# Summing the modulation's partitions with ones as the weights, and the products moved to the front of the mixers' stage

## The reference, cut to what matters

```python
for l in range(DEPTH):                                   # DEPTH = 2
    mod = cond @ ada_w[l] + ada_b[l]                     # 1024 -> 6 * 1024
    sh1, sc1, g1, sh2, sc2, g2 = jnp.split(mod, 6, axis=-1)
    h = rms_norm(x, norm1_g[l]) * (1.0 + sc1) + sh1
    pa, pb, pc, pd = split(h @ w_in[l], GROUP_COLS)
    y = concatenate([rwkv7(pa), diff_attention(pb), spatial_gating(pc), forgetting_attention(pd)])
    x = x + g1 * (y @ w_out[l])
    h = rms_norm(x, norm2_g[l]) * (1.0 + sc2) + sh2
    x = x + g2 * conv_glu_ffn(h)
...
mod = silu(c) @ w_mod + b_mod                            # second block: the same for a GLA mixer
x = x + g1 * gla(h, h_ctx)
x = x + g2 * moe(modulate(rmsnorm(x), sh2, sc2))
```

## Time and profile before

| | |
|---|---|
| Median of 3 runs | 2577.76 us (2577.53 to 2583.84) |
| Profiled execution, its own time | 2571.56 us |
| Its span in the trace | 2569.8 us |
| PE busy | 2306.9 us (90%) |
| PE weight loads busy | 1853.0 us (72%) |
| DVE busy | 1598.1 us (62%) |
| ACT busy | 1067.6 us (42%) |
| POOL busy | 177.1 us (7%) |

### The profile page before, as it was taken

One profiled execution on the slowest core, in us unless ns is written; L12 is line 12 of the kernel. 1 busy time (PEld: TensorE's weight loads), 2 busy tenths in 40 slices (PEclk: granted clock), 3 DMA queues, 4 the chain that ended last, 5 costly groups with the idle time before them and its releaser, 6 DMA issues. The chain is left out here.

```text
span 2569.8 us, 32135 instructions
## 1 busy us (share of the span) xinstructions
PE 2306.9 (90%) x11490; PEld 1853.0 (72%) x11490; DVE 1598.1 (62%) x2270; ACT 1067.6 (42%) x1616; POOL 177.1 (7%) x201
## 2 busy tenths in 40 slices
PE   4998689799999999877989999999998888799995
PEld 3777566578888777756657888788877776677774
DVE  6654656555567565565655555774643655699996
ACT  3443244333342234242343333423333434577774
POOL 0001100000000000111000000000000101123232
PEclk8998899999999999799989999998999999899997
DMA  7640000222225355100012223445624001799995
GB/s 295 219 164 5 1 34 1 78 79 97 90 100 188 112 196 190 44 1 1 34 42 75 97 90 101 153 150 182 210 92 164 1 1 43 291 397 397 396 397 213
DMA packets 95240, 348.22 MB, mean 136 GB/s; under 512 B 12288, under 2 KB 14352, under 8 KB 94864
## 3 DMA queue, kind: packets, MB, share of 16 engines
q1 hardware_dynamic: 88496, 323.57, 35.4%
q0 software_dynamic: 3888, 14.16, 1.4%
q10 hardware_dynamic: 2736, 8.92, 0.9%
HBM read 333.50 MB, written 21.50 MB: 138 GB/s over the span
## 5 line engine op out<-in xcount | busy, mean ns | idle before, releaser
L498 PE MATMUL ps<-a_hi,w_hi 128*128 128x512 f32 x1408 | 572.8, 407 | 41.6 <-DVE y_lo L1775 18.4
L500 PE MATMUL ps<-a_hi,w_lo 128*128 128x512 f32 x1408 | 564.6, 401 | 0.0
L499 PE MATMUL ps<-h_lo,w_hi 128*128 128x512 f32 x1280 | 508.2, 397 | 0.0
L462 DVE TENSOR_TENSOR w_lo<-ring,w_hi 128x1024 fp32r<-128x1024 f32 x178 | 218.1, 1226 | 384.3 <-ACT w_hi L457 383.9
L457 ACT ACTIVATE w_hi<-ring 128x1024 fp32r<-128x1024 f32 x178 | 188.3, 1058 | 532.8 <-PE ps L500 520.1
L498 PEld LDWEIGHTS ps<-a_hi,w_hi 128*128 128x128 f32 x1408 | 268.9, 191 | 115.7 <-DVE w_lo L462 28.4
L500 PEld LDWEIGHTS ps<-a_hi,w_lo 128*128 128x128 f32 x1408 | 268.5, 191 | 66.6
L499 PEld LDWEIGHTS ps<-h_lo,w_hi 128*128 128x128 f32 x1280 | 243.7, 190 | 60.9 <-issue 2.9
L3150 DVE TENSOR_TENSOR moe_w_lo<-p,moe_w_hi 128x1024 fp32r<-128x1024 f32 x187 | 247.1, 1365 | 12.9 <-ACT moe_w_hi L3249 11.6
L3249 ACT ACTIVATE moe_w_hi<-p 128x1024 fp32r<-128x1024 f32 x204 | 216.0, 1062 | 66.9 <-PE ps L3192 60.5
L1998 PE MATMUL ps<-p_lo,down_hi 128*128 128x512 f32 x352 | 137.8, 392 | 0.0
(11 more groups left out here) (632 smaller groups left out, 4253.0 us busy)
## 6 DMA issues: line engine op xcount, KB each, us to landing
ring<-in_ffn_up SPq DMA_DIRECT2D x88, 512.0 KB, 3.4
ring<-in_w_in SPq DMA_DIRECT2D x72, 512.0 KB, 5.2
p<-in_moe_gate SPq DMA_DIRECT2D x68, 512.0 KB, 6.2
p<-in_moe_up SPq DMA_DIRECT2D x68, 512.0 KB, 5.6
p<-in_moe_down SPq DMA_DIRECT2D x68, 512.0 KB, 7.2
vt<-in_ada SPq DMA_DIRECT2D x64, 512.0 KB, 4.0
p<-in_ada SPq DMA_DIRECT2D x48, 512.0 KB, 5.7
down_raw<-in_ffn_down SPq DMA_DIRECT2D x32, 704.0 KB, 5.0
```

The costliest lines, as they stand in the source:

```text
L462: self.c.nc.vector.tensor_tensor(self.c.w_lo[:, s % 2, :], self.c.slot(s), self.c.w_hi[:, s % 2, :].bitcast(F32), ALU.subtract).then_inc(s ...
L498: nc.tensor.matmul(bank, c.w_hi[:, s % 2, at], hi(kt), start=(kt == 0), stop=False)
L499: nc.tensor.matmul(bank, c.w_hi[:, s % 2, at], lo(kt), start=False, stop=False)
L500: return nc.tensor.matmul(bank, c.w_lo[:, s % 2, at], hi(kt), start=False, stop=(kt == KT - 1))
```

## The change

Three things change. The partition sum is turned around: a block of ones (128 x 64) is the weight, and the accumulator moves through, 512 columns at a time. Each quarter takes two such products, one for each half of its 1024 columns; the first half's sum fills rows 0 to 63 of a bank (64 equal rows), the second half's rows 64 to 127. ACT copies the bank to SBUF. The result is now in rows, so it has to be turned: SP writes row 0 and row 64 of each copy to a small tensor in memory (8 transfers of 2 KB), reads it back as 32 partitions x 128 columns (one transfer), PE transposes that once (32 columns), and DVE adds the bias to all 32 columns.

In `mixers` the eight products and four ACT copies stand in one step right behind rwkv's first, ahead of `prepare(0)`; the turn and the bias stand after attention's `prepare` and rwkv's `intra(0)`, ahead of the forgetting attention. In `gla_heads` each head has two products and a copy in the old place, and the turn and the bias come once, three steps ahead of the last head's end.

```diff
-def modulation_stream(c, name, sums, bank, quarters_in_order):
+class ModRows:
+    HALF = 64
+    def __init__(self, c, name, ada, rows, bank_of, turn_bank):
+        ...
+        self.tile = c.small2[0:ada.count * KT, 0:P]
+    def sum_quarter(self, j):
+        acc = self.ada.sums[0][1][j]
+        for half in range(2):
+            last = self.c.nc.tensor.matmul(self.bank_of(j)[half * self.HALF:(half + 1) * self.HALF, :],
+                                           self.c.const("ones", self.HALF), acc[:, half * S:(half + 1) * S], start=True,
+                                           stop=True)
+        last.then_inc(self.summed, 1)
+    def copy_quarter(self, act, j):
+        act.wait_ge(self.summed, j + 1)
+        self.c.nc.scalar.activation(self.rows(j), self.bank_of(j), ACT.Copy).then_inc(self.copied, 1)
+    def spread(self, sp):
+        row_dram = self.c.dram["mod_rows"]
+        sp.wait_ge(self.copied, self.ada.count)
+        for j in range(self.ada.count):
+            for half in range(2):
+                at = slice(half * self.HALF, half * self.HALF + 1)
+                sp.dma_start(row_dram[2 * j + half:2 * j + half + 1, :], self.rows(j)[at, :]).then_inc(self.stored, 16)
+        sp.wait_ge(self.stored, 32 * self.ada.count)
+        sp.dma_start(self.tile, row_dram.rearrange("a (t p) -> (a t) p", p=P)).then_inc(self.loaded, 16)
+    def turn(self, pe):
+        n = self.ada.count * KT
+        pe.wait_ge(self.loaded, 16)
+        self.c.nc.tensor.transpose(self.turn_bank[:, 0:n], self.tile, self.c.const("ident")[0:n, 0:n]).then_inc(self.turned, 1)
+    def add_bias(self, dve):
+        n, dst = self.ada.count * KT, self.ada.dsts[0]
+        dve.wait_ge(self.ada.bias, 16)
+        dve.wait_ge(self.turned, 1)
+        self.c.nc.vector.tensor_tensor(dst, self.turn_bank[:, 0:n], dst, ALU.add).then_inc(self.ada.biased, 1)
...
 def mixers(c, sums, w_out, ahead):
-    modulation = modulation_stream(c, "mod", sums, A_BANK + 3, (2, 0, 1, 3))
+    mod = ModRows(c, "mod", sums, lambda j: c.vt[:, j // 2, j % 2 * S:(j % 2 + 1) * S], lambda j: c.ps[:, A_BANK + j, :],
+                  c.ps[:, A_BANK + 3, :])
-    plan = [1] * b["shift"] + [0] * a["first"] + [1, 1, 2, 2, 1, 2, 2, 1]
-    plan += alternate(a["gating"] + a["prepare"], b["intra"])
+    plan = [1] * b["shift"] + [2] + [0] * a["first"] + [1, 1, 1, 1]
+    plan += alternate(a["gating"] + a["prepare"], b["intra"]) + [2]
...
             att["sp"]()
+            modulation["sp"]()
             rw["sp"]()
```

More of the change, by code:

```diff
@@ L605, in units, with attention_stream @@
         v=lambda i, n=1: flat[:, i * S:(i + n) * S])
-def attention_stream(c, sums, nc):
+def attention_stream(c, mod, nc):
     at = units(c)
@@ L720, in pe @@
         yield
-        eng.wait_ge(sums.biased, 1)
+        eng.wait_ge(mod.copied, mod.ada.count)
         for t in range(2):
@@ L1662, in _ @@
                 early(t)
-def modulation_stream(c, name, sums, bank, quarters_in_order):
+class ModRows:
+    HALF = 64
+    def __init__(self, c, name, ada, rows, bank_of, turn_bank):
+        self.c, self.ada, self.rows, self.bank_of, self.turn_bank = c, ada, rows, bank_of, turn_bank
+        self.summed, self.copied, self.stored, self.loaded, self.turned, ada.biased = (
+            c.sem(f"{name}_{n}") for n in ("summed", "copied", "stored", "loaded", "turned", "biased"))
+        self.tile = c.small2[0:ada.count * KT, 0:P]
[27 more added lines that the diff above has]
+        self.c.nc.vector.tensor_tensor(dst, self.turn_bank[:, 0:n], dst, ALU.add).then_inc(self.ada.biased, 1)
@@ L1667, in modulation_stream @@
+def modulation_stream(c, mod, turned_after):
     nc = c.nc
-    finish_sums, finish_bias = adaln_finish_parts(c, name, sums, bank=bank)
     def pe():
-        for j in quarters_in_order:
-            finish_sums(nc.tensor, parts=[j])
-            yield
+        for j in range(mod.ada.count):
+            mod.sum_quarter(j)
+        yield
+        nc.tensor.wait_ge(*turned_after)
+        mod.turn(nc.tensor)
+        yield
     def act():
-        for j in quarters_in_order:
-            yield
+        for j in range(mod.ada.count):
+            mod.copy_quarter(nc.scalar, j)
+        yield
+        yield
@@ L1679, in dve @@
     def dve():
[L1680 to L1685, removed]
+        yield
+        mod.add_bias(nc.vector)
+        yield
+    return dict(pe=pe, act=act, dve=dve, sp=lambda: mod.spread(nc.sync), steps=2)
 def mixers(c, sums, w_out, ahead):
     nc = c.nc
-    modulation = modulation_stream(c, "mod", sums, A_BANK + 3, (2, 0, 1, 3))
@@ L1692, in mixers @@
-    att = attention_stream(c, sums, nc)
+    mod = ModRows(c, "mod", sums, lambda j: c.vt[:, j // 2, j % 2 * S:(j % 2 + 1) * S], lambda j: c.ps[:, A_BANK + j, :],
+                  c.ps[:, A_BANK + 3, :])
+    att = attention_stream(c, mod, nc)
+    modulation = modulation_stream(c, mod, att["roped"])
     rw = rwkv_stream(c, att, w_out, nc)
     a, b = att["steps"], rw["steps"]
-    plan = [1] * b["shift"] + [0] * a["first"] + [1, 1, 2, 2, 1, 2, 2, 1]
-    plan += alternate(a["gating"] + a["prepare"], b["intra"])
+    plan = [1] * b["shift"] + [2] + [0] * a["first"] + [1, 1, 1, 1]
@@ L2788, in gla_heads, with copy_parts @@
                                             "ms", "rs", "ended")}
-    summed, sums.biased = c.sem("b2_mod_summed"), c.sem("b2_mod_biased")
-    prep = gla_prepare_stream(c, w, gates, pr, sn, sums.biased)
+    mod = ModRows(c, "b2_mod", sums, lambda j: sums.sums[0][1][j][:, 0:S], lambda j: c.ps[:, 0, :], c.ps[:, 0, :])
+    prep = gla_prepare_stream(c, w, gates, pr, sn, mod.copied)
     scan = gla_scan_stream(c, w, pr, sn, fill, filled, w_out)
     def sum_parts():
[L2794 to L2797, removed]
+        for j in range(sums.count):
+            mod.sum_quarter(j)
             yield
+        mod.turn(nc.tensor)
+        yield
+    def copy_parts():
+        for j in range(sums.count):
+            mod.copy_quarter(nc.scalar, j)
+            yield
+        yield
     def add_bias():
-        nc.vector.wait_ge(sums.bias, 16)
         for j in range(sums.count):
-            dst = sums.dsts[0][:, j * KT:(j + 1) * KT]
-            nc.vector.wait_ge(summed, j + 1)
-            nc.vector.tensor_tensor(dst, c.ps[:, 0, 0:KT], dst, ALU.add).then_inc(sums.biased, 1)
             yield
-    modulation = dict(pe=sum_parts, dve=add_bias, act=lambda: iter([None] * sums.count))
+        mod.add_bias(nc.vector)
+        yield
+    modulation = dict(pe=sum_parts, dve=add_bias, act=copy_parts)
     streams = [scan, prep, modulation]
@@ L2818, in _ @@
             scan["sp"]()
+            mod.spread(sp)
         @block.gpsimd
```

14 lines of the change are left out of this document (10 added, 4 removed).

## The result

| | before | after |
|---|---|---|
| Median of 7 runs, same session | 2572.42 us (2563.70 to 2583.84) | 2550.67 us (2543.57 to 2555.49) |
| Ratio, 95% interval | | 0.9905 (0.9886 to 0.9924) |
| Profiled execution, its own time | 2571.56 us | 2546.32 us |
| Clock granted to TensorE, mean over the span | 0.946 | 0.962 |

The kernel is faster by 21.8 us between the medians. The gain forecast, 19.7 us, is a ratio of 0.9923 and lies inside the interval, but the time forecast, 2558 us, and its lower end, 2552, were too high. A second session with six more runs of the changed kernel gave 2554.70 us against 2572.06 for before, 0.9928 (0.9912 to 0.9943). All 13 runs of after have a mean of 2552.1 us, all 38 of before (the three shown at the start and 35 beside the experiments) 2573.7: a gain of 21.6, plus or minus 2.7.

The account below looks back on a forecast made before the run. PE's narrow modulation sums, stalling DVE in program order, were taken to bound the front; 17.1 + 3.1 - 0.5 = 19.7 us gain, so 2551.9 profiled and 2558 median, range 2552 to 2570.

Parts of the forecast that it names:

- What bounds the front, and what goes: Mixers' front: DVE waits at the bias for PE's narrow sums; removing this gives 7.0 and 10.1 us, 17.1 in all.
- The products: Mixers' front: eight products, halves side by side at full clock, take 3.4 us; late ACT is paid by faster L1140.
- The rivals on order and clock: Mixers' front and GLA: halves run one after the other (10%, 2569 us); products get the low clock (6%, 2566.5); both (4%, 2584).
- The first round: L1168's 32 records in the mixers: no difference taken, bounds over both layers -5.1 to +1.7 us.
- the clock takes it back: Rival, mixers: PE's idleness keeps the low clock through the first two rounds and gating; gain only 8 us, 2570 (4%).
- The turn: Store, read back, transpose and bias: 0.25 us a layer, 0.5 in all; nothing in GLA; DVE's L1710 wait below 0.5.
- GLA: GLA heads: two products side by side replace L2796's sums; gain 1.3 + 3 x 0.6 = 3.1 us.
- The level: Whole kernel: the median of the runs lies 6.2 us above the profiled execution, so 2551.9 becomes 2558.
- The range: Whole kernel, 8 in 10: 2552 to 2570 us, reaching up to the first three rivals.

Follow-up runs that it names:

- e4: Changed kernel, but with 64 narrow one-column sums in their old place, one small copy, no turn, bias still late: L1122 to L1172 takes 23.36 and 26.45 us.
- e3: Changed kernel with the wide products back in the narrow sums' old place on PE and ACT's copies behind its second prepare step: 2555.77 us, ratio 0.9912.
- e9: Changed kernel with ACT's copies behind its second prepare step, then eight extra products per layer on PE, results unused: 2546.45 us, ratio 0.9907.
- e10: Label not defined in the text; apparently the changed kernel run again unaltered, for a second trace and its spread: 2554.70 us, ratio 0.9928.
- e6: Changed kernel with the eight products reordered, four upper halves first, then four lower: products take 5.42 us, L1122 to L1172 takes 20.29 us in both layers.
- e8: Changed kernel with two quarters' products at the front and the other two, with their copies, behind the gating's turns L725: 2549.90 us, ratio 0.9895.
- e5: Changed kernel, but with narrow one-column sums at the front, one small copy and the bias late: L1122 to L1172 takes 26.13 and 26.25 us.

## Why the prediction was right and wrong

- **What bounds the front, and what goes: right.** DVE's wait is gone, and L1172 starts 18.55 and 18.54 us after L1122, where 18.5 was forecast. The working named the second wait behind the first ("what L1385 needs of PE (L1144) comes right after L1140 now") and took it as gone, which the wide products make true. e4 gives its size: with the bias moved and the narrow sums left, it keeps 4.8 of the 6.9 us and 7.9 of the 10.0. The place at the front added nothing to F: e3, with the old place, has 18.31 and 18.50.
- **The products: right.** Side by side, 3.65 us for 3.4 plus the tail, from 194.71, at the full clock. L1283 is 1.2 us late, L1144 faster by 0.75, and L1368 starts at 202.57, forecast 202.4. The rivals on order and clock are out.
- **The first round: right within its bounds.** 6.39 and 6.59 us, where 5.44 and 6.70 stood: 0.8 us lost, inside the -5.1 to 1.7. That it comes out near nothing is in part luck: the third trace of before has 3.81 us in the first layer, after a wait of PE like that before the 5.44 us in the other two (1.9 to 2.1 us). What could be had is -4.5 us, as e9 shows with 3.81 in each layer. Of the rival "the clock takes it back" only these 0.8 us came: from 217 to 226 us the granted clock is 1.00 in the changed kernel.
- **The turn: right in the mixers; in GLA the wait was missed.** In both layers DVE adds the bias without idle time before it; in GLA's last head (the second row below) it waits 1.50 us for the transposed rows, where less than 0.5 us of idle time was forecast. The read back had been issued at 2075.03, and PE ran L2762 without a pause until its transpose at 2090.52, so DVE waited for PE's program order and not for the transfers. PE idles 0.51 us for ACT right behind it, as forecast, and no cost of this wait shows. ACT's value copies start 5.9 us earlier than before (L880 at 237.2, L876 at 243.1), with the layer, so the store was not in their way. DVE in the changed kernel:

```profile
269.12 0.18 DVE L1710 TENSOR_TENSOR mod<-ps,mod 128x32 f32<-128x32 f32 x1
...
2090.87 0.19 DVE L1710 TENSOR_TENSOR mod<-ps,mod 128x32 f32<-128x32 f32 x1 [1.50 <-PE ps L1704]
```

- **GLA: mis-sized.** 3.1 forecast, 4.9 measured against like traces. The term for the products was near: 1.90 us for 2.0 in the first head and 1.01 for 1.1 in the others, where 3.28 and 1.70 stood, so 3.4 us on PE's own lines. The matched points of like traces are 4.6 and 4.3 us apart by the last head's end, 6.8 and 6.3 by 2200 us, and 5.2 and 4.8 by 2240, where part is given back. From 1945 to 2200 us the granted clock is 0.91 before and 0.94 and 0.93 in the same stretch of the two traces of after, so low clock can be part of the 1.5 us that PE's own lines don't explain; whether it is, and whether it follows from the edit, was not tested, and this part of the cause stays open.
- **The level: wrong, and it is the step that put the forecast outside.** "The median of the runs is 6.2 higher, so 2558." That level rested on three runs at 2577.53, 2577.76 and 2583.84. With four more, the median was 2572.42, and over 38 runs before has a mean of 2573.7, 2.2 above the profiled execution and not 6.2. Of the 7.4 us between 2558.1 and the measured 2550.67, 5.3 are this level (2577.76 against 2572.42) and 2.0 are gain, about as much as GLA's term was too small. From a level of 2573.7 the same gain gives 2554.0, and the range, shifted by as much, 2548 to 2566. That the 2551.9 forecast for the profiled execution is so near the mean of 13 runs of after (2552.1) is luck: the level 2.2 too low and the gain 1.9 too small cancel.
- **The range: too narrow, because one source was missing.** Its terms were all costs of this change. The same kernel scatters by itself, with a standard deviation of 4.3 us (after) and 4.6 (before), and e10 shows the places. The working had the 7.7 us that the measurement can't tell from no change, but used them for the chance of "faster" alone. By an estimate from these deviations, medians of three and of seven runs are good to some 3.3 and 2.0 us (1.25 times the deviation over the root of the number), so the range needed 4 us and more on both sides before any term of the change.

## What to carry over

A reduction over partitions by one-column products costs its weight loads, here 0.16 to 0.21 us each, and PE looks fully busy while the granted clock falls to 0.50 (layer 1) or stays there (layer 2): swap the operands so that the accumulator moves and the ones stay, and put two such products side by side on the halves of the array. Test a change of place by itself: here the wide products gained as much in the old place. When an instruction is moved off an engine's path, look for the second wait behind it, since PE's order may hold the same consumer. Take a kernel's level from as many runs as the gain asks for, and read the gain of a change from matched instructions in two traces of *each* kernel, since two executions of one kernel can lie 9 us apart in a stretch that nobody touched.

## What was not expected of the hardware

- Products on different halves of the output partitions overlap even when they are not neighbours: the first lower record, ninth in the program's order, started beside the fifth upper one, ahead of three that stand before it (e6).
- Idle gaps of PE cost twice. Filling one of 4.5 us with products whose results nobody reads shortened the 32 records behind it from 6.4 to 3.8 us (e9), although the fillers themselves ran partly at half clock (16 records in 5.17 us for 3.65). The round took 3.81 to 3.84 us in all four layers of e8 and e9, and 3.88 and 4.27 in e4, where PE did not wait before it; in the other traces, with 1.9 us and more of idle time before it, it took 5.1 to 6.8 us, but for the one of 3.81 in the third trace of before. So the gap makes the low clock likely and not certain.
- DVE's L1364 takes 0.85 to 0.92 us in most traces, and 4.46 in the first of after, 4.54 in e3 and, in the second layer, 4.48 in e5 (there L1362). POOL in the changed kernel:

```profile
196.53 3.65 POOL L1109 MEMSET h<- 128x512 f32 x5
```

  L1364 starts before that burst, at 196.00, and ends behind it, at 200.46. Where it takes 0.87 us, in the first trace of before, it overlaps a like burst too (from 196.44), so what decides is open. It cost nothing here, since DVE waits for L1144 until 202.5 anyway.
